# ScalarE rounds u in the first MLP quarter, the rest of u moves behind a weight half, and two down groups are copied to y by ScalarE

## The reference, cut to what matters

```
h = rms_norm(x, norm2_g) * (1 + scale2(c)) + shift2(c)
x = x + gate2(c) * (square(relu(h @ W1)) @ W2)      # W1 2048x8192, W2 8192x2048
out = rms_norm(x, final_g)
```

## Time and profile before

| what | value |
|---|---|
| median of 3 runs | 1156.21 us (1155.56 to 1156.94) |
| the profiled execution | 1155.3 us |
| its span, first to last instruction | 1153.5 us |
| busy share of the span: TensorE, VectorE, ScalarE | 97%, 85%, 57% |
| mean granted TensorE clock | 0.989 of full speed |

### The profile page before, as it was taken

One profiled execution on the slowest core, in us unless ns is written; L12 is line 12 of the kernel. 1 busy time (PEld: TensorE's weight loads), 2 busy tenths in 40 slices (PEclk: granted clock), 3 DMA queues, 4 the chain that ended last, 5 costly groups with the idle time before them and its releaser, 6 DMA issues.

```text
span 1153.5 us, 19470 instructions
## 1 busy us (share of the span) xinstructions
PE 1116.0 (97%) x7945; PEld 1029.0 (89%) x7945; DVE 981.2 (85%) x1213; ACT 658.8 (57%) x962; POOL 36.1 (3%) x52
## 2 busy tenths in 40 slices
PE   4999999999999999999999999999999999999996
PEld 4899999999887778999789999989999989999885
DVE  5998999988997998997888787988778988867685
ACT  6655448977775556545554445665445555455452
POOL 1000000000000000001000000000000000000000
PEclk6999999999999999999999999999999999999998
DMA  9999998878975798995555775588775688767441
GB/s 377 419 419 421 421 411 320 272 213 255 351 282 220 282 319 311 382 382 197 208 187 232 311 272 204 200 243 301 291 280 183 208 259 286 305 225 276 156 183 73
DMA packets 50832, 321.15 MB, mean 278 GB/s; under 512 B 6764, under 2 KB 8632, under 8 KB 14264
## 3 DMA queue, kind: packets, MB, share of 16 engines
q1 hardware_dynamic: 44592, 305.72, 69.0%
q0 software_dynamic: 4256, 11.55, 5.7%
q10 hardware_dynamic: 1896, 2.64, 0.8%
HBM read 305.20 MB, written 4.21 MB: 268 GB/s over the span
## 4 chain that ended last, share of the span: by engine, by line
PE 68%; DVE 16%; DMA 6%; ACT 5%; issue 4%; SPq 0%; ACTq 0%; DVEq 0%
PE quad L1342 12%; PE quad L1344 12%; PE quad L1343 12%; PE quad L1355 8%; PE quad L1357 8%; PE quad L1356 8%; DVE w_lo L1911 4%; DMA first_raw<-in_w_mod 3%; DVE mod_raw L1918 2%; PE quad L1401 2%; PE quad L1403 2%; PE quad L1402 2%; DVE first_raw L1918 2%; DMA y<-stage 2%; DMA mod_raw<-in_w_mod 2%
## 5 line engine op out<-in xcount | busy, mean ns | idle before, releaser
L947 ACT ACTIVATE w_hi<-raw 128x1024 fp32r<-128x1024 f32 (+1 forms) x332 | 344.1, 1042 | 253.6 <-PE quad L1344 163.1
L1911 DVE TENSOR_TENSOR w_lo<-raw,w_hi 128x1024 fp32r<-128x1024 f32 (+1 forms) x332 | 395.5, 1203 | 94.0 <-ACT w_hi L947 93.4
L1342 PE MATMUL quad<-act,w_hi 128*128 128x256 f32 x1528 | 426.7, 279 | 5.9 <-DVE w_lo L1911 3.8
L1343 PE MATMUL quad<-act,w_hi 128*128 128x256 f32 x1528 | 424.5, 278 | 0.0
L1344 PE MATMUL quad<-act,w_lo 128*128 128x256 f32 x1528 | 424.5, 278 | 0.0
L1342 PEld LDWEIGHTS quad<-act,w_hi 128*128 128x128 f32 x1528 | 288.1, 189 | 8.6 <-issue 4.6
L1343 PEld LDWEIGHTS quad<-act,w_hi 128*128 128x128 f32 x1528 | 289.4, 189 | 0.2
L1344 PEld LDWEIGHTS quad<-act,w_lo 128*128 128x128 f32 x1528 | 288.1, 189 | 0.0
L1355 PE MATMUL quad<-w_hi,u_hi 128*128 128x512 f32 x336 | 132.0, 393 | 1.1 <-DVE u_lo L2369 1.0
L1357 PE MATMUL quad<-w_hi,u_lo 128*128 128x512 f32 x336 | 131.1, 390 | 0.0
L1356 PE MATMUL quad<-w_lo,u_hi 128*128 128x512 f32 x336 | 130.7, 389 | 0.0
(11 more groups left out here) (369 smaller groups left out, 1699.6 us busy)
## 6 DMA issues: line engine op xcount, KB each, us to landing
raw<-in_w_main SPq DMA_DIRECT2D x184, 1024.0 KB, 6.2
mod_raw<-in_w_mod SPq DMA_DIRECT2D x67, 1024.0 KB, 7.8
first_raw<-in_w_mod SPq DMA_DIRECT2D x14, 1024.0 KB, 15.8
late_raw<-in_w_mod SPq DMA_DIRECT2D x10, 1024.0 KB, 8.1
acc<-in_w_mod SPq DMA_DIRECT2D x4, 1024.0 KB, 12.3
conv_b<-conv_q POOLq DMA_DIRECT2D x8, 512.0 KB, 5.6
y<-stage POOLq DMA_DIRECT2D x6, 512.0 KB, 8.9
shared<-stage POOLq DMA_DIRECT2D x6, 512.0 KB, 5.3
```

What stands on the lines that cost most here:

```text
L947: A(dst[:, 0:2 * width], block_half(raw, j, width), ACT.Copy).then_inc(hi_done, 1)
L1342: mm(out, hi, act_hi[:, k, :], start=begin and m % 2 == 0, stop=False, skip_group_check=True)
L1343: mm(out, hi, act_lo[:, k, :], start=False, stop=False, skip_group_check=True)
L1911: TTn(lo[:, 0:2 * width], block_half(raw, j, width), hi[:, 0:2 * width].bitcast(f32), ALU.subtract)\
```

## The change

In the first quarter alone, three things change.

1. ScalarE rounds u to `u_hi`, at n = 33+2i, between its wait for the square and the copy to `u_keep`; the VectorE copy is gone.
2. On VectorE the rest of u becomes a function of its own, `first_rest(i)`, called behind the low part of weight half 33+2i, where it was called ahead of it.
3. The copies of column groups 0 and 1 to `y` move from VectorE to ScalarE, at the same n = 44 and 52, under a new semaphore `evac_first`. `down_sum` is gone, and counts of `evac_dve` fall by two.

```diff
# ScalarE
                     if n == relu_half(i) + 1 and i < N_SPLIT:
                         act.wait_ge(u_step, 2 * i + 1)
+                        A(u_hi[:, 4 * i:4 * i + 4, :], relu[:, :].rearrange("p (k t) -> p k t", k=4), ACT.Copy)\
+                            .then_inc(u_step, 1)
                         A(u_keep[i][:, :], relu[:, GW:2 * GW], ACT.Copy).then_inc(u_kept, 1)
...
+                if n % 8 == 4 and n // 8 in (5, 6):
+                    cg = n // 8 - 5
+                    act.wait_ge(pe_half, half_end(0, 4 + cg, HALVES - 1))
+                    A(y[:, :, cg * GW:(cg + 1) * GW], pair[2 * cg][:, :].rearrange("p (t n) -> p t n", t=TT), ACT.Copy)\
+                        .then_inc(evac_first, 1)
# TensorE
-                        pe.wait_ge(evac_dve, 4 + 3)
+                        pe.wait_ge(evac_dve, 4 + 1)
...
-                    pe.wait_ge(evac_dve, 4 + cg - 1)
+                    pe.wait_ge(evac_first, cg - 1)
# VectorE
             def first_square(i):
 
-                tiles = slice(4 * i, 4 * i + 4)
-                r3 = relu[:, :].rearrange("p (k t) -> p k t", k=4)
                 dve.wait_ge(up_used, i + 1)
                 TTn(relu[:, :], relu[:, :], relu[:, :], ALU.mult).then_inc(u_step, 1)
-                dve.wait_ge(u_step, 2 * i + 1)
-                v.tensor_copy(u_hi[:, tiles, :], r3).then_inc(u_step, 1)
+
+            def first_rest(i):
+
+                tiles = slice(4 * i, 4 * i + 4)
                 dve.wait_ge(u_step, 2 * i + 2)
-                if i < N_SPLIT:
-                    dve.wait_ge(u_kept, i + 1)
-                TTn(u_lo[:, tiles, :], r3, u_hi[:, tiles, :].bitcast(f32), ALU.subtract).then_inc(u_ready, 1)
+                dve.wait_ge(u_kept, i + 1)
+                TTn(u_lo[:, tiles, :], relu[:, :].rearrange("p (k t) -> p k t", k=4), u_hi[:, tiles, :].bitcast(f32),
+                    ALU.subtract).then_inc(u_ready, 1)
...
-                    else:
-                        down_sum(0, cg, first=True)
...
                     weight_lo(G_MLP + i, j, kind=BY_FEATURE if i < 4 else BY_TOKEN)
+                for i in range(4):
+                    if n == relu_half(i) + 1:
+                        first_rest(i)
```

More of the change, by code:

```diff
@@ L576, in build @@
         staged = sem("staged")
+        evac_first = sem("evac_first")
         stage_added = sem("stage_added")
@@ L589, in build @@
         N_STAGED = 3
-        EVAC_DOWN = 8 + len(SPLIT_QUARTERS)
+        EVAC_DOWN = 6 + len(SPLIT_QUARTERS)
         def stage_count(q, cg, part):
@@ L865, in staged_sums @@
                 pool.wait_ge(staged, stage_count(q, cg, 0))
-                if q == 1:
-                    pool.wait_ge(evac_dve, 4 + cg + 1)
+                if q == 1 and cg < 2:
+                    pool.wait_ge(evac_first, cg + 1)
+                elif q == 1:
+                    pool.wait_ge(evac_dve, 4 + cg - 1)
                 pool.dma_start(y[:, :, cols], stage[:, :].rearrange("p (t n) -> p t n", t=TT), accum_op=ALU.add)                    .then_inc(stage_added, 16)
@@ L1858, in mlp_up @@
                     elif i == 0:
-                        pe.wait_ge(evac_dve, 4 + 3)
+                        pe.wait_ge(evac_dve, 4 + 1)
                     elif i == 2:
-                        pe.wait_ge(evac_dve, 8 + q - 1)
+                        pe.wait_ge(evac_dve, 6 + q - 1)
                     up_group(q * 8 + G_MLP + i, i)
@@ L2381, in up_rest @@
                     u_hi[:, tiles, :].bitcast(f32), ALU.subtract).then_inc(u_ready, 1)
[L2383 to L2388, removed]
-                else:
-                    dve.wait_ge(evac_dve, q * 4 + (cg + 1))
-                    TTn(y[:, :, cols], y[:, :, cols], bank3[cg], ALU.add).then_inc(evac_dve, 1)
             def split_sum(q, cg):
@@ L2400, in split_sum @@
                 if q > 0:
-                    dve.wait_ge(evac_dve, 8 + q - 1)
+                    dve.wait_ge(evac_dve, 6 + q - 1)
                 TTn(shared[:, cg, :], shared[:, cg, :], bank[:, 2 * GW:4 * GW], ALU.add).then_inc(shared_sum, 1)
```

## The result

The changed kernel takes 1170.74 us in the median (1168.85 to 1175.51, 4 runs) against 1156.58 us before: a ratio of 1.0123, 95% interval 1.0102 to 1.0144. It is slower, by 14.2 us. The profiled execution took 1168.85 us, its span is 1167.1 us, 13.6 more than before. The forecast was +13.5 us and 1169.7.

A forecast was written before the change was run, and what follows sets the result against it. TensorE was taken to bound the kernel, with no idle time behind the first MLP quarter. Profiled 1155.3 us + 12.0 (ring) + 1.5 (clock) = 1168.8, and 0.9 more for the median: 1169.7 us; range 1166.5 to 1172.5.

The forecast's parts named there:

- The bound: TensorE has no idle time behind the first MLP quarter, so its delay near 550 us reaches the end in full.
- Rival C: TensorE's lost time is given back later, behind 560 us: anything between 1158 and 1166 us; chance 0.06.
- The turn of nine steps, 9.45: First quarter, ReLU to next ReLU: nine instructions must follow one another, 9.45 us a turn against 6.46 before.
- the ring: First quarter: four groups reuse one relu buffer, each ReLU waiting for the previous u; its slowing costs +12.0 us.
- The rounding on ScalarE against that on VectorE: Rounding u in each turn: 0.97 us on ScalarE to its next instruction, where VectorE's cast took 0.74.
- The y copies at nothing: The two copies to y on ScalarE at n = 44 and 52: price 0; uncovered up to 1 us each.
- The clock: TensorE's clock falls in 3.7 us stalls; only the last restart costs the end, 0 to 2.75 us, taken as 1.5.
- Rival A: The ring slows as forecast but TensorE's clock is kept: +12.0 us, 1168.2 us; chance 0.32.
- B: TensorE's low clock lasts over both last restarts and bounds a turn: +16.5 to +18 us, 1173 to 1174; chance 0.07.
- a spared fall: Middle turns: a slow start shortens TensorE's next stall, to as little as 1.1 us, which may spare a clock fall.
- Rival D: Odd half rounded before the square is done: turn about 5.7 us, 1.3 us won, 1154.9 us; chance 0.05.
- The sum: Whole kernel: profiled 1155.3 + 12.0 + 1.5 = 1168.8 us, plus 0.9 for the median: 1169.7 us.

The follow-up runs named there:

- experiment 3: Changed kernel with u rounded on VectorE as before, the rest of u still behind the odd half's low part: 1167.08 us, ratio 1.0083.
- experiment 4: Changed kernel with the rest of u put back ahead of the odd weight half's low part on VectorE: 1161.86 us, ratio 1.0033.
- experiment 5: Changed kernel with the odd weight half's rounding on ScalarE moved ahead of the wait for the square: 1161.29 us, ratio 1.0028.
- experiment 2: Kernel before, with only the two copies to y moved to ScalarE: 1156.72 us, ratio 0.9997.
- experiment 6: Changed kernel plus 14 extra TensorE matmuls ahead of the wait for u in each of halves 34, 36 and 38: 1175.19 us, ratio 1.0148.
- experiment 8: Changed kernel plus 14 extra TensorE matmuls ahead of each of halves 34, 36 and 38, a repeat run: 1173.47 us, ratio 1.0153.
- experiment 9: Changed kernel plus 14 extra TensorE matmuls ahead of half 38 alone: 1171.88 us, ratio 1.0126.
- experiment 7: Changed kernel run again without edits, on the same chip as the run with extra matmuls: 1170.48 us, ratio 1.0109.
- experiment 10: Changed kernel run once more without edits, beside two runs with extra matmuls: 1171.22 us, ratio 1.0122.
- experiment 11: Kernel before, with square, rounding and rest of u moved ahead of the even half's low part on VectorE: 1155.04 us against 1157.23, ratio 0.9981.
- experiment 1: Changed kernel with the two copies to y left on VectorE: 1172.43 us, ratio 1.0124.

## Why the prediction was right

Read by its own steps:

- **The bound.** TensorE has nothing to give back behind 560 us. Holds: the shift of 13.96 us that stands at the second quarter's ReLUs (649.45 to 663.41) still stands at the last of the third quarter's (886.24 to 900.20), 0.54 of it from ahead of the change. Rival C is out.
- **The turn of nine steps, 9.45.** It is 9.41 in every run of the change. The step from `u_keep` to the odd half was 0.52, not 0.54, and two weight steps 1.07 and 1.08, not 1.09. The restart of half 38 moved 11.83 us, forecast 11.98. Experiments 3 to 5 took pieces of the ring out and gave 8.47, 7.40 and 7.40 where the same sum said 8.49, 7.33 and 7.33.
- **The rounding on ScalarE against that on VectorE.** 0.97 to the next instruction, as taken. That the sum falls from 9.41 to 8.47 with VectorE's cast is this 0.97, less 0.03. By the Trainium skill (ScalarE: Activation LUTs, "What ACT_TABLE_LOAD costs") the estimate was 0.95, and the 0.97 of the trace agrees.
- **The y copies at nothing.** Confirmed by experiment 2.
- **The clock.** Priced at 1.5 us between bounds of 0 and 2.75; it was 1.58, 1.61, 1.38 and 1.58 in the four profiled executions with the full ring and no extra matmuls (their Q less the 129.78 of experiments 6 and 8). The 1.5 was a choice near the middle of a wide range, and that it came within 0.1 us is luck. The bound of 2.75 rested on one rise of 5.5 us. In middle turns the low clock lasted up to 6.0 us behind a restart (experiment 9), so the bound was not safe; behind the last restart it lasted 2.9 to 3.9 us. That a fall in a middle turn is free, and only the last restart pays, was argued, and experiments 3 and 9 show it. Rival A is out, and so is B: no low stretch lasted over both last restarts. What was foreseen as possible, a spared fall, is the rule in the runs: the falls alternate. A fall at the restart of half 34 shortens the next stall to 1.19 us, so the restart of half 36 keeps its clock and the last has a full stall in front of it again.
- **Rival D.** Its condition, the odd half rounded before the wait, is what experiment 5 made true. Even so the turn was 7.40 and not 5.7, because the rest of u also waits for `u_keep` on ScalarE and since the cast's 0.74 was replaced by ScalarE's 1.68 to the rest. As priced, D was too low by 1.7 us a turn: it would have come out at +3.8 us in Q and not at −1.3.
- **The sum.** Forecast +13.5, Q +13.4, profiled executions +13.6, medians +14.2. The changed kernel's runs spread over 6.7 us. The forecast had no term for what varies outside the first quarter; with only three runs of before, 1.4 us apart, it was not to be seen, and in 19 and 23 later runs the kernel before spread over 6 us too. Since Q repeats within 0.2 us, the spread must come from elsewhere, and the profiled executions show where it can: the start of the first ReLU (up to 4.3 us), the second quarter (up to 2.6), the third (up to 9.3) and the fourth (2.6, once). Which of these make the last 0.6 us of the medians is open; the timed runs have no trace. In experiments 7 and 10 the whole change's median lay 13.3 and 13.5 us above that of the kernel before.

## What to carry to other kernels

Before an instruction with a wait is put in front of others on an in-order engine, write down the ring that the wait closes, and add up every instruction that the order now forces between the release and the next wait; an engine's busy share of the whole span does not show it (ScalarE is busy for 57% before and after). The place of a few instructions moved this kernel's turn from 6.46 to 9.41 us, and in experiment 11 to 5.40. Then check the engine with the most work in a turn: when the ring is short, its own work sets the turn, as VectorE's did in experiment 11. And the last stall of a ring may cost more than its length, since TensorE may start slowly behind it, here for 1.4 to 1.6 us; slow starts in the turns before cost nothing here, since the next stall was shorter by as much.

## What the runs showed of the hardware

The granted clock fell at each of the nine stalls of TensorE of 3.6 or 3.7 us that the profiled executions of the change and experiments 1, 7, 9 and 10 have, at the one of 3.3 us in the third quarter of experiment 8, and at one of the two of 2.7 us in experiment 3. It did not move with the one stall of 2.1 us (experiment 7), with those of 1.2 to 1.7 us, three each in experiments 4 and 5, nor with the pauses of 0.5 us that the extra matmuls left. It could fall inside the stall, the earliest 2.2 us behind the last matmul (at 549.3 in the change), or after TensorE had started again: 0.2 us behind the restart at 569.65 in the change, 1.3 us behind the one at 551.13 in experiment 7. The low stretches of these stalls ended 2.9 to 6.0 us after the restart. The Trainium skill (TensorE: Matmul & The Clock Gate, "HAM oscillation — how this bites in real kernels") tells of a stall in front of each burst and a slow start of each; here every second burst started slowly: a slow burst left a stall of 0.9 to 2.1 us behind it, and none of these brought a fall.
